# Expert loop of an encoder block: the down weights' loads issued from ScalarE's queue in place of SyncE's

## What is computed

```python
def expert_block(args):
    xblk, e = args
    a = xblk @ w_gate[e]
    u = xblk @ w_up[e]
    return (jax.nn.silu(a) * u) @ w_down[e]
```

## Time and profile before

| | us |
|---|---|
| median of 3 runs | 1721.01 |
| the profiled execution | 1722.2 |
| span of its profile | 1720.6 |
| TensorE busy (matmuls) | 1562.0 |
| VectorE busy | 1349.0 |
| ScalarE busy | 690.0 |
| GpSimd busy | 359.3 |

### The profile page before, as it was taken

The page is one execution under the profiler, slowest core; times in us unless marked ns, Lnnn a source line. Parts: engine busy times, 40 slices in busy tenths (PEclk is TensorE's granted clock), DMA queues, the critical chain, the costliest instruction groups (busy, mean ns, idle before and its releaser), DMA issues.

```text
span 1720.6 us, 21491 instructions
## 1 busy us (share of the span) xinstructions
PE 1562.0 (91%) x6992; PEld 1279.0 (74%) x6992; DVE 1349.0 (78%) x1149; ACT 690.0 (40%) x581; POOL 359.3 (21%) x217
## 2 busy tenths in 40 slices
PE   2799999999999999899989957999999999999971
PEld 2688888888888888677768845788877777777761
DVE  5777869797787877986454456999999989999984
ACT  4401111111201113244122134677776767666752
POOL 1100000000000010000000002445545544444440
PEclk9999999999999999899989957999999999999995
DMA  7414223231423325345244246999999999999935
GB/s 254 141 62 134 85 85 110 98 110 61 134 66 105 110 85 178 117 148 158 87 152 158 96 171 249 364 368 370 375 359 357 355 358 360 351 354 368 368 113 209
DMA packets 167574, 352.11 MB, mean 205 GB/s; under 512 B 17228, under 2 KB 90956, under 8 KB 167541
## 3 DMA queue, kind: packets, MB, share of 16 engines
q1 hardware_dynamic: 150838, 309.71, 50.6%
q0 software_dynamic: 16704, 41.98, 8.1%
HBM read 323.84 MB, written 46.66 MB: 215 GB/s over the span
## 4 chain that ended last, share of the span: by engine, by line
PE 62%; DMA 18%; DVE 11%; issue 4%; ACT 4%; POOL 1%; DVEq 0%; SPq 0%; POOLq 0%; ACTq 0%
PE ps L1281 19%; PE ps L1283 19%; PE ps L1282 19%; DMA e_raw<-in_w_down_dram 14%; DVE e_lo L1209 3%; ACT e_hi L756 2%; DMA xg<-d_h,g_idx 2%; DVE e_lo L1205 2%; DVE conv_acc_b L963 1%; DVE macc L869 1%; PE ps L1421 1%; PE ps L1473 1%; PE ps L1345 1%; DVE f_o L1271 1%; DMA prow<-in_c_dram 0%
## 5 line engine op out<-in xcount | busy, mean ns | idle before, releaser
L1281 PE MATMUL ps<-A_hi,w_hi 128*128 128x512 f32 x1024 | 400.7, 391 | 4.2 <-DVE A_lo L899 4.2
L1282 PE MATMUL ps<-A_lo,w_hi 128*128 128x512 f32 x1024 | 399.6, 390 | 0.0
L1283 PE MATMUL ps<-A_hi,w_lo 128*128 128x512 f32 x1024 | 399.4, 390 | 0.0
L1205 DVE TENSOR_TENSOR e_lo<-e_raw,e_hi 128x2048 fp32r<-128x2048 f32 x136 | 308.9, 2284 | 12.3 <-ACT e_hi L750 10.9
L963 DVE SCALAR_TENSOR_TENSOR conv_acc_b<-glu,colc,conv_acc_b 128x1024 f32<-128x1024 f32 x232 | 298.0, 1285 | 10.2 <-DVE rows L948 0.5
L750 ACT CAST e_hi<-e_raw 128x2048 fp32r<-128x2048 f32 x136 | 259.7, 1912 | 61.1 <-PE ps L1283 55.6
L1281 PEld LDWEIGHTS ps<-A_hi,w_hi 128*128 128x128 f32 x1024 | 193.0, 188 | 45.2 <-issue 4.4
L1282 PEld LDWEIGHTS ps<-A_lo,w_hi 128*128 128x128 f32 x1024 | 193.0, 188 | 40.5 <-issue 0.5
L1283 PEld LDWEIGHTS ps<-A_hi,w_lo 128*128 128x128 f32 x1024 | 193.0, 188 | 40.2
L1281 PE MATMUL ps<-e_hi,xT_hi 128*128 128x512 f32 x528 | 212.5, 402 | 0.0
L1283 PE MATMUL ps<-e_hi,xT_lo 128*128 128x512 f32 x528 | 206.9, 392 | 0.0
(11 more groups left out here) (236 smaller groups left out, 2041.1 us busy)
## 6 DMA issues: line engine op xcount, KB each, us to landing
e_raw<-in_w_gate_dram SPq DMA_DIRECT2D x132, 512.0 KB, 6.0
e_raw<-in_w_up_dram SPq DMA_DIRECT2D x132, 512.0 KB, 12.4
e_raw<-in_w_down_dram SPq DMA_DIRECT2D x66, 1024.0 KB, 13.9
w_raw<-in_w_in_dram SPq DMA_DIRECT2D x56, 512.0 KB, 4.3
stream<-in_w_ada_dram SPq DMA_DIRECT2D x48, 512.0 KB, 5.6
xn<-in_x_dram SPq DMA_DIRECT2D x8, 512.0 KB, 7.0
d_short<-conv_acc_a POOLq DMA_DIRECT2D x8, 512.0 KB, 4.0
d_gate_a<-gate_st POOLq DMA_DIRECT2D x8, 512.0 KB, 2.9
```

Source lines behind the costliest of these rows:

```text
L1205: v.tensor_tensor(e_lo[:, q, :], e_raw[:, q, :], e_hi[:, q, :].bitcast(F32), ALU.subtract).then_inc(gu_lo, 1)
L1281: t.matmul(dst, st_hi, mv_hi, start=first, stop=False)
L1282: t.matmul(dst, st_hi, mv_lo, start=False, stop=False)
L1283: return t.matmul(dst, st_lo, mv_hi, start=False, stop=last)
```

## The change

The down chunks of block b are now loaded by ScalarE's queue, in its own iteration b, after `x_hi` and before the first `gu_split`; the lines that did it are gone from SyncE. The expert number is read from the table by ScalarE. The waits are on the same counts of `d_lo`: with b on ScalarE one more than b on SyncE, `b * 2 + (q - 1)` is the same number. Block 0's down chunks are still loaded by SyncE ahead of the loop.

```diff
@@ SyncE, loop over b @@
                         for q in range(4):
                             sp.wait_ge(gu_lo, b * 4 + (4 + q + 1))
                             sp.sem_inc(e_full[q], 32)
-                    e_down = expert_of(b + 1)
-                    for q in range(2):
-                        held(d_lo, b * 2 + (q + 1))
-                        load_down(q, e_down)
@@ ScalarE, loop over b @@
                     with act.If(b < n_blk):
                         x_hi(1 - par, b + 2)
+                        e_down = act.value_load(tab[0:1, bass.ds(b, 1)], min_val=0, max_val=NE - 1)
+                        for q in range(2):
+                            act.wait_ge(d_lo, b * 2 + (q - 1))
+                            src = w_down[bass.ds(e_down, 1), 2 * q * P:2 * (q + 1) * P, :].rearrange("a (k p) n -> p (a k) n", p=P)
+                            act.dma_start(e_raw[:, 4 + q, :].rearrange("p (k n) -> p k n", k=2), src).then_inc(e_full[4 + q], 16)
                         for q in range(2):
                             gu_split(q, b * 32 + 64, b * 4 + (q + 1))
                         h_hi(b)
```

## The result

The changed kernel takes 1734.8 us, the median of 5 runs (1732.62 to 1735.76), against 1721.01: a ratio of 1.0074, 95% interval 1.0061 to 1.0086 (the ratio is not the bare quotient of the two medians, which is 1.0080). It is slower by 0.7%. The profiled execution took 1732.62 us, 10.4 more than the one of before.

What follows compares the result with a forecast made beforehand. TensorE was taken to limit early blocks, DMA backlog late ones; after the change, VectorE's 17.45 us cycle plus a 1.66 us hold. 31 x 0.37 = 11.5 us plus 2, on 1722.2, gives 1735.7, stated as 1735; range 1724 to 1753.

Steps and rivals of the forecast that it cites:

- VectorE's least cycle, 17.45 us, plus the hold: Expert loop: VectorE's block without idle time, 17.45 us, plus 1.66 us idle while ScalarE waits for chunk 1's buffer: 19.11 us.
- Rival B: ScalarE's hold is under 1.5 us, or DMA backlog decides most blocks: 18.8 to 19.0 us a block, 1727; chance 0.17.
- The start of the cast: ScalarE, from down chunk 1's issue to the first gate/up cast's start: 0.15 us taken, bounds 0 to 0.8.
- Chunk 0's issue 1.0 to 2.0 us late: Down chunk 0's load, behind x_hi and the table read on ScalarE, goes 1.0 to 2.0 us later; taken as costing nothing.
- The sum: Whole loop: cycle rises from 18.74 to 19.11 us, 31 x 0.37 = 11.5 us; with 2 us added, 1735.7.
- The 2 us added: Allowance on top of the loop's 11.5 us, for blocks where DMA still wins and the first iteration's hold.
- The late part paced by DMA: Late blocks take 19.29 us because of DMA backlog; almost none of the hold shows there, 19.11 being less.
- Short backlog: Longer cycle keeps the DMA queue short: from 8.5 us it grows under 0.2 us a block, some 5 over the loop.
- the 13 allowed: About 13 us may pass from down chunk 0's issue to its landing before VectorE would be delayed.
- Two queues: SyncE's and ScalarE's queues are served in turn, changing service order; sum kept, since loads have slack while backlog is short.
- rival A: Down loads on ScalarE's queue overtake gate/up loads wanted first: 20.0 us a block, 39 us more, 1760; chance 0.13.
- Rival C: Faster: down loads land before wanted, late blocks run at 18.20 us, 22 us gained, 1699; needs hold under 0.75; chance 0.05.

## Why the prediction was right

The forecast was 1735 us and slower; 1734.8 was measured, and the mechanism is the one named: ScalarE's stop ahead of the first cast, 1.52 us of idle time on VectorE in every block. That the number is met to 0.2 us is luck. The profiled execution was forecast at 1735.7 and took 1732.62; 11.5 us were worked out for the loop and 10.4 came, and 2 us were added that no trace shows. By its steps:

- *VectorE's least cycle, 17.45 us, plus the hold.* Right. From the end of down chunk 1's low part: to the issue 0.15 us (predicted 0.24), the issue 0.39, to the cast 0.18 (0.15), the cast 1.91, to VectorE 0.03: 2.66 against 2.72. The cycle is 19.08 against 19.11. Rival B drew its line at a hold of 1.5 us and 19.0 us a block, so it was missed by little.
- *The start of the cast*, the term with the widest bounds (0 to 0.8), lay at 0.18, where the gap between two issues on SyncE had put it; the modelled end of a matmul was no measure for it.
- *Chunk 0's issue 1.0 to 2.0 us late.* Wrong: it goes 0.24 us after y_out's start, where on SyncE it went at 0.31. VectorE's preceding low part (1332.26 + 2.29) ended at 1334.55 and the issue began at 1334.70. The table read started at 1333.7, beside the cast of 1332.70 to 1334.62.
- *The sum.* 31 x 0.34 = 10.4 us, against 11.5. The 2 us added for blocks in which DMA still wins and for the first iteration's hold have next to no place in the trace: all steps are 19.1 us, and the first y_out starts 0.5 us later. The medians differ by 13.8 us, the profiled executions by 10.4; the profile shows only the latter.
- *The late part paced by DMA.* Half right. The waits for landings were there, but 19.29 us was no floor: halved down bytes brought 9 us, not 18, and all bytes on the same queue were served at 18.55 in another order of VectorE's work. The prediction had the late part lose almost nothing; it gained 2.8 us, and the rest of the loop lost 13.2. The sum came out since it went by the average, 18.74, which holds both. Why the late steps before were as long as 19.29 stays open.
- *Short backlog.* Right: down landings went from 9.6 us (early) to 11.3, by medians, and the longest of the loop took 12.8, just under the 13 allowed.
- *Two queues.* The Trainium skill, "DMA: Bandwidth & Descriptors", section "Queues, rings and completion order", has each DMA engine take turns between SyncE's row and ScalarE's. The landings agree with that, though none shows the turns themselves: with chunk 0 alone on ScalarE's queue waits for up loads rose to 39.5 us, and down loads issued late took 10.1 us there where in SyncE's queue they took 8.2. In the changed kernel it cost nothing that shows, so rival A was right to be a rival and not the forecast; its price, 1760, was seen nowhere.
- *Rival C* failed where it said it would: its condition was a hold under 0.75 us. The down waits did go, and 1.52 us a block came in their place.

## What to carry to other kernels

Before moving a load to a compute engine's queue, write down what stands behind its wait there: the engine stops at a wait for a buffer to come free, and in a loop that is balanced to a microsecond the work behind it pays. Here the same queue with one cast moved ahead of the wait was 12 us faster than the change. Waits for DMA in one part of a loop do not mean that a hold is hidden in the rest. Here the part with these waits gained 2.8 us, and the steps without them, 18.2 us and less, lost more than that. Add up the steps part by part before going by an average.

## What the runs showed of the hardware

- An issue of a 1 MB load on ScalarE's queue takes 0.39 us, as on SyncE's (0.386); two issues of 512 KB take 0.84 together, and that lengthened the loop by 0.46 us a block.
- Two loads of 1 MB issued 0.55 us apart on ScalarE's queue, beside gate/up loads on SyncE's, were cast 5 us apart, each cast released by its landing (1433.25 and 1438.40).
